# A two-layer hybrid decoder step on eight cores: the program is recorded as a graph and put in order by a list scheduler, the residual becomes token-major, gate sums are scanned

## The reference

```python
for l in range(2):
    hn = rms_norm(h, norm_mix)                       # h: tokens x 1024
    q,k,v,g_out,g_lr,xp,u,vv,gates = split(hn @ w_in)    # 7696 columns
    # A: gated linear attention, 4 heads, state 128 x 256 per head
    g_log = log_sigmoid(g_lr @ w_gk2 + b_gk) / 16
    b = cumsum(g_log)                                # inside a chunk of tokens
    o = (q*exp(b)) @ S + tril((q*exp(b)) @ (k*exp(-b)).T) @ v
    S = exp(b_last) * (S + (k*exp(-b)).T @ v)
    A = (rms_norm(o) * silu(g_out)) @ w_br_a
    # B: trailing window means (2, 4, 8, 16) minus the token, a map per group
    # C: u * (tril(W_s) v + b) in chunks of 128
    h = h + (sig(ga)*A + sig(gb)*B + sig(gc)*C) @ w_out
    h = h + relu(rms_norm(h) @ w_ff1)**2 @ w_ff2     # d_ff = 4096
y = rms_norm(h)
```

## Time and profile before

| | us |
|---|---|
| runs of the kernel (3) | 2885.13, 2886.05, 2887.64; median 2886.05 |
| profiled execution, slowest core (core 4), first to last instruction | 2896.9 |
| spans of the 8 cores in it | 2877.6 to 2896.9 |
| PE busy / its weight loads | 2545.4 (88%) / 1384.2 (48%) |
| DVE / ACT / POOL busy | 1237.7 (43%) / 929.9 (32%) / 75.3 (3%) |
| DMA, HBM read and written | 237.46 MB and 63.96 MB |

### The profile page before, as it was taken

One profiled execution on the slowest core, in us unless ns is written; L12 is line 12 of the kernel. 1 busy time (PEld: TensorE's weight loads), 2 busy tenths in 40 slices (PEclk: granted clock), 3 DMA queues, 4 the chain that ended last, 5 costly groups with the idle time before them and its releaser, 6 DMA issues.

```text
span 2896.9 us, 42207 instructions; the slowest of 8 cores (2877.6 to 2896.9 us)
## 1 busy us (share of the span) xinstructions
PE 2545.4 (88%) x14347; PEld 1384.2 (48%) x14502; DVE 1237.7 (43%) x2227; ACT 929.9 (32%) x1698; POOL 75.3 (3%) x94
## 2 busy tenths in 40 slices
PE   5767967899997899999986797797999889999997
PEld 3434544454543455455443454454455435555554
DVE  4244336434444444444544433553343444444443
ACT  4335545312222211122334454541222231111243
POOL 1000000000000000000000000000000000000000
PEclk6889988999999999999998899898999999999998
DMA  9743071432626211214343307133162621211011
GB/s 242 129 129 112 12 116 44 93 104 62 126 77 134 44 30 30 44 16 81 73 104 113 117 23 110 46 70 115 59 129 77 135 59 16 44 30 30 15 45 80
DMA packets 172520, 225.73 MB, mean 78 GB/s; under 512 B 12242, under 2 KB 159866, under 8 KB 166904
## 3 DMA queue, kind: packets, MB, share of 16 engines
q0 software_dynamic: 80896, 77.97, 19.2%
q1 hardware_dynamic: 91416, 145.06, 15.7%
HBM read 237.46 MB, written 63.96 MB: 104 GB/s over the span
## 4 chain that ended last, share of the span: by engine, by line
PE 77%; DMA 10%; DVE 5%; ACT 4%; issue 3%; SPq 1%; another core or an unknown queue 0%; DVEq 0%; ACTq 0%
PE ps L215 75%; DMA hst<-spool 2%; DMA gla_s<-Sf_77 1%; DVE hn L194 1%; DMA gla_s<-Sf_78 1%; DMA gla_s<-Sf_76 1%; PE ps L224 1%; DMA gla_s<-Sf_79 1%; DMA xt_55<-xp 1%; DMA H4s_110<-H_d 1%; SPq L164 1%; ACT L188 1%; DVE tmp_86 L194 0%; ACT rstd L188 0%; DVE pt_101 L191 0%
## 5 line engine op out<-in xcount | busy, mean ns | idle before, releaser
L215 PE MATMUL ps<-hn,wring 128*128 128x384 bf16 (+1 forms) x6320 | 1251.0, 351 | 13.4 <-DMA wring<-w_in 8.6
L215 PEld LDWEIGHTS ps<-hn,wring 128*128 128x128 bf16 x6400 | 628.0, 99 | 555.3 <-issue 28.8
L188 ACT ACTIVATE rl_124<-ps 128x384 f32<-128x384 f32 (+1 forms) x160 | 85.3, 533 | 502.3 <-PE ps L215 439.8
L215 PE MATMUL ps<-a_1_123,wring 128*128 128x384 bf16 (+1 forms) x1268 | 245.1, 348 | 0.6
L215 PE MATMUL ps<-a_0_122,wring 128*128 128x384 bf16 (+1 forms) x1267 | 241.0, 347 | 0.7
L215 PE MATMUL ps<-wring,hn 128*128 128x512 bf16 x819 | 198.4, 390 | 9.8 <-ACT lv L188 4.1
L215 PEld LDWEIGHTS ps<-a_1_123,wring 128*128 128x128 bf16 x1280 | 125.3, 98 | 108.3 <-issue 2.2
L215 PEld LDWEIGHTS ps<-a_0_122,wring 128*128 128x128 bf16 x1280 | 125.0, 98 | 108.0
L188 ACT ACTIVATE sg_119<-ps 128x384 f32<-128x384 f32 (+1 forms) x120 | 64.0, 533 | 263.8 <-PE ps L215 193.2
L188 ACT ACTIVATE sg_118<-ps 128x384 f32<-128x384 f32 (+1 forms) x120 | 64.0, 533 | 226.4 <-PE ps L215 167.8
L188 ACT ACTIVATE rl_125<-ps 128x384 f32<-128x384 f32 (+1 forms) x160 | 85.3, 533 | 146.3 <-PE ps L215 83.8
(11 more groups left out here) (311 smaller groups left out, 2835.4 us busy)
## 6 DMA issues: line engine op xcount, KB each, us to landing
wring<-w_ff POOLq DMA_DIRECT2D x32, 1024.0 KB, 9.1
wring<-w_in POOLq DMA_DIRECT2D x30, 1024.0 KB, 12.7
OB_d<-OBC SPq DMA_DIRECT2D x6, 768.0 KB, 4.1
H4s_110<-H_d SPq DMA_DIRECT2D x6, 768.0 KB, 12.4
OBs_112<-OB_d SPq DMA_DIRECT2D x6, 768.0 KB, 14.2
H4s_111<-H_d SPq DMA_DIRECT2D x6, 768.0 KB, 13.8
OBs_113<-OB_d SPq DMA_DIRECT2D x6, 768.0 KB, 5.5
h_d<-hT_47 SPq DMA_DIRECT2D x2, 2048.0 KB
```

The source lines that it names most:

```text
L188: return op(ACT, lambda: nc.scalar.activation(out=out, in_=in_, func=func, **kw), reads, writes)
L215: inst = nc.tensor.matmul(m[0], m[1], m[2], start=m[3], stop=m[4], **kw)
```

## The change

Every helper (`act`, `tt`, `pe_group`, `dma` ...) no longer emits its instruction but appends a node to a graph (`record`), with the buffers it reads and writes, a duration and a latency. The code is then written in plain program order without generators, and `schedule()` emits the nodes: again and again, over the five engines, it takes the node that can start first; among those of an engine that can start within 30 ns the one recorded first (an ACT node that needs another table set counts as 60 places later). PSUM banks are given out there too, all eight from one pool.

```diff
-    def op(E, fn, reads=(), writes=()):
-        acquire(E, reads, writes)
-        t = E.tok(fn())
+    def schedule():
+        ...
+                for n in ready[id(E)]:
+                    s = n.ready if n.ready > f else f
+                    key = n.idx
+                    ...
+                    c = (max(s, f + 30.0), key)
+            ...
+            if n.byts:
+                ...
+                dma_at[id(E)] = at0 + (both + alone / 280.0 if alone else n.byts / 140.0)
+                fin = dma_at[id(E)] + 2000.0
```

```diff
+    def rstd_of(src, srcB, junk):
+        act(junk.t[:, :], src, AF.Square, srcB, [junk, s], accum=s.t[:, 0:1])
+        act(s.t[:, 0:1], s.t[:, 0:1], AF.Ln, [s], [s], bias=EPS, scale=1.0 / D)
+        act(s.t[:, 0:1], s.t[:, 0:1], AF.Exp, [s], [s], scale=-0.5)
+    def norm_to_hn(t, src, srcB, junk, stage):
+        s = rstd_of(src, srcB, junk)
+        stt(stage.t[:, :], src, s.t[:, 0:1], wn.t[:, :], ALU.mult, ALU.mult, list(srcB) + [s, wn], [stage])
+        pe_transposes([...  for kt in range(KT)], ident_bf.t[:, :], [stage, ident_bf], [ps])
+        vcopy(hn_v(b)[:, :, j * 128:(j + 1) * 128], ...)
-            pe_group([(ps.t[:, 0:T], ones_bf.t[:, :], s.t[:, 0:T], m == 0, m == KT - 1)], [s, ones_bf], [ps])
```

```diff
-                pe_group([(ps.t[:, j * 128:(j + 1) * 128], lv.t[:, j, h * 128:(h + 1) * 128], cm.t[:, mi, :], True, True)], ...)
+            op(DVE, lambda: nc.vector.tensor_tensor_scan(out=x.t[:, 0:T], data0=rst.t[:, m0:m0 + T], data1=x.t[:, 0:T], initial=0.0,
+                                                         op0=ALU.mult, op1=ALU.add), [x, rst], [x], 2 * T / 0.96 + 90.0, 90.0)
-        plq.dma(wgk2.t[0:16, :], w_gk2[l], writes=[wgk2])
-        plq.dma(wgk2.t[32:33, :], b_gk[l:l + 1, :], writes=[wgk2])
+        for j in range(4):
+            plq.dma(wgk2.t[32 * j:32 * j + 16, :], w_gk2[l], writes=[wgk2])
-            act(sb_.t[:, :, :], s.t[:, :, :], AF.Copy, [s], [sb_])
+                vcopy(sb_.t[:, :, :], s.t[:, :, :], [s], [sb_], E=POOL)
-    Sf = [sba(f"Sf{i}", [128, 2, 256], F32, RA + (6 + 2 * i) * KB) for i in range(4)]
+    Sf = [sba(f"Sf{i}", [128, 2, 256], F32, at(86 + 2 * i)) for i in range(5)]
```

More of the change, by code:

```diff
@@ L96, in release, with __init__ @@
         b.r = {}
+class P(B):
+    def __init__(self, ps_t, allowed):
+        B.__init__(self)
+        self.allowed = allowed
+        self.k = None
+        self.left = 0
+        self.last = 0.0
+        self.t = Late(lambda: ps_t[:, self.k or 0, :])
+class Node:
+    __slots__ = ("E", "fn", "reads", "writes", "late", "occ", "lat", "aset", "idx", "succ", "need", "ready", "tiles", "byts")
 def build_program():
@@ L148, in build_program, with record @@
     POOL = Eng(nc, nc.gpsimd, "pool")
+    nodes = []
+    def record(E, fn, reads, writes, occ, lat, late=(), aset=None, byts=0):
+        n = Node()
+        n.E, n.fn, n.reads, n.writes, n.late = E, fn, tuple(reads), tuple(writes), tuple(late)
+        n.occ, n.lat, n.aset, n.byts = occ, lat, aset, byts
+        n.idx = len(nodes)
+        n.succ = []
+        n.ready = 0.0
+        before = {}
+        for b in n.reads + n.late:
+            for a in b.overlap():
+                if a.lw is not None:
+                    before[a.lw.idx] = a.lw
+        for b in n.writes:
+            for a in b.overlap():
+                if a.lw is not None:
+                    before[a.lw.idx] = a.lw
+                for m in a.lr:
+                    before[m.idx] = m
+        for b in n.reads + n.late:
+            b.lr.append(n)
+        for b in n.writes:
+            b.lw = n
+            b.lr = []
+        before.pop(n.idx, None)
+        n.need = len(before)
+        for m in before.values():
+            m.succ.append(n)
+        n.tiles = list({id(b): b for b in n.reads + n.writes + n.late if isinstance(b, P)}.values())
+        for b in n.tiles:
+            b.left += 1
+        nodes.append(n)
@@ L243, in ps_release @@
[L243 to L271, removed]
-            bg.remove(e)
+            aps += not isinstance(scale, float)
@@ new lines, in act, with vcost, tt @@
+        if accum is not None:
+            kw["accum_out"] = accum
+            aps += 2
+        occ = 0.833 * cols(out) + (60.0 if in_psum(*reads) else 110.0) + 95.0 * aps
+        op(ACT, lambda: nc.scalar.activation(out=now(out), in_=now(in_), func=func, **kw), reads, writes, occ, 125.0, SETS.get(func))
+    def vcost(out, reads, rate=1.0):
+        return cols(out) / 0.96 / rate + 85.0
+    def tt(out, in0, in1, alu, reads, writes, E=None):
+        E = E or DVE
+        occ = vcost(out, reads) if E is DVE else 250.0 + 2.2 * cols(out)
+        op(E, lambda: E.e.tensor_tensor(out=now(out), in0=now(in0), in1=now(in1), op=alu), reads, writes, occ, 90.0)
@@ new lines, in memset, with fn @@
+    def memset(ap, v, writes, E=None):
+        E = E or DVE
+        op(E, lambda: E.e.memset(ap, v), (), writes, vcost(ap, ()), 90.0)
+    def pe_group(mms, reads, writes, late=None):
+        def fn(rs, ws, lt):
+            acquire(PE, rs, ws)
+            inst = None
+            for i, m in enumerate(mms):
+                kw = {}
+                if len(m) > 5 and m[5]:
+                    kw["skip_group_check"] = True
+                if late is not None:
+                    for a in lt[i].overlap():
+                        PE.wait(a.w)
+                inst = nc.tensor.matmul(now(m[0]), m[1], m[2], start=m[3], stop=m[4], **kw)
+            release(PE.tok(inst), list(rs) + list(lt), ws)
+        occ = 0.0
+        for m in mms:
+            n = cols(m[2])
+            occ += max(n / 2.4 * (4 if m[2].dtype == F32 else 1) + 2.5, 60.0)
+        record(PE, fn, reads, writes, occ, 190.0, late=late or ())
@@ L720, in o_view @@
[L720 to L736 removed]
+    cnt2 = [0]
@@ L1099, in build_program @@
-        while smp_e in bg:
-            tick()
+                gla_sample(l)
         mix_prep(l)
```

1089 lines of the change are left out of this document (515 added, 574 removed).

## The result

The changed kernel takes 2517.99 us (median of 5 runs) against 2887.64 (also 5). The ratio is 0.8709, 95% interval 0.8676 to 0.8743. A second set of runs gave 2518.65 us and 0.8696 (0.8684 to 0.8708). The forecast was 2545, with 2475 to 2700 as the range. In some executions the cores of one die run at a lower clock throughout; the first two medians count these, the ratios and every time from here on leave them out.

A forecast was written before the change was run, and what follows sets the result against it. PE-bound in gates and FF, held up by waits elsewhere, 482 us lost. Work 2348 plus losses 60, 37, 64, 6, 8, 6, 7 and 20 gave 2556 us of span, less 10.8: 2545 us, range 2475 to 2700.

The forecast's parts named there:

- Work: PE's work over the whole kernel: from 2415 us, less 97 removed, plus 30 for new bf16 transposes, to 2348 us.
- Start: Loading x and the first weight chunks: DMA-bound at 242 GB/s until 95 us, PE losing 60 us (45 to 80).
- Sample loop and scans: Mixers: PE loses 15 and 22 us in the two layers' sample loops, and 32 us a layer in scans.
- the scans' term: Scans of blocks 2, 3 and 4: DVE's work exceeds PE's, losing 32 us a layer (15 to 50).
- pace: Time between states in the sample loop: DMA sets it, 2.2 us at its bound, 2.5 taken, 2.2 to 2.6 expected.
- Gates, Out, FF: Remaining PE losses in these stages, both layers: 3 us each in gates, 4 each in Out, 6 in FF together.
- Tail: After the last product: only an add, the norm and one store remain, 7 us.
- Clock: Where PE idles its granted clock falls; the mixers stay below 1.00, costing 20 us (5 to 40).
- Rival 1: Waits stay because the build-time order meets late DMAs: 2819 us if all, about 2690 if half; over 2700 chance 0.11.
- sample loop at today's pace: Bound for the sample loop if states come as slowly as before, 3.8 us each: 60 and 67 us lost.
- POOL's cast: Rival 2: the sample loop's cast on POOL sets the pace and slows the kernel, needing 7.8 us a cast; chance 0.02.
- The clock did not give way: Rival 3: dense running on all eight cores lowers PE's clock; time passes 2886 us at share 0.87; chance 0.02.

The follow-up runs named there:

- six buffers: Changed kernel with six state buffers in the sample loop's rotation instead of five, two tiles moved to make room: 2525.1 us, ratio 0.8751.
- flat durations: Changed kernel, scheduler counting 0.5 us per ACT, DVE and SP instruction and multiples of 0.9 us for product groups and POOL: 2645.0 us, ratio 0.9174.
- altered DMA rule: Changed kernel, scheduler counting 3.0 us and 230 GB/s per transfer instead of 2.0 us and 280 GB/s: 2534.84 and 2538.45 us.
- 100 steps: Changed kernel, PE, ACT and DVE at most 100 recorded steps ahead of their own oldest unplaced instruction: 2589.9 us, ratio 0.8973.

## Why the prediction was right, and what was wrong in it

The direction and the mechanism held: PE's work fell as computed, and the waits in gates, Out and FF went. Its sum of 2556 us of span was 39 too long: work 16 too small, clock 25 too small, idle time 80 too large. That these errors have different signs is luck. So is that the time is off by only 27 (2545 against 2518). The sum took off 10.8 us because the profiled execution of before was that much above its median; that belonged to this one execution, and the profiled span of the changed kernel lies 1.3 us below its time.

What the prediction named as signs came: mixers until 453.5 us and 386.5 us long (forecast 460 and 390), gates 294 (297), Out 66 (70), FF 483 and 474 (480), the clock in Out 1.00, the first ring load at 23.2 us (27).

- **Work**, 2348 forecast, 2364 measured, although the narrow gate, which I had priced at full columns, saves some 13 us by itself. What I left out of the price is thus near 30 us; no run says which products they are.
- **Start**, 60 us lost forecast, 47 measured: PE idled 45 of the first 95 us and had done 48 us of work (50.11 x 0.96), where I had put 35. The DMA engines were busy 0.99 of it, as said, but at 186 GB/s, not 242, and PE's last wait for the ring ended at 83.6 us, not 95. The sum behind the 95 mixes two counts: 12.6 MB are six chunks as read, in float32, while the profile's MB and GB/s count what lands, and there a chunk is 1.05 MB. What q0, the casting queue, lands costs more of the engines' time: 7.64 MB in 64.8% of 95 us are 124 GB/s by estimate, q1's 9.93 MB in 33.6% 311 GB/s (113 and 289 in the first 76.7 us of the kernel before, by the rows below). Six chunks, 6.3 MB, at 124 GB/s take 51 us, and 12.6 MB at 242 take 52: two errors that cancelled. The wait for the row copies was there, and it cost nothing.

```profile
q1 hardware_dynamic: 3904, 16.16, 73.0%
q0 software_dynamic: 3389, 2.36, 27.3%
```

- **Sample loop and scans**, 47 us of idle time forecast for layer 0 and 54 for layer 1; measured 18.1 + 11.9 = 30 and 24.7. The step that failed is the scans' term, "42 us of PE work in all against 65 of DVE", 32 us a layer: from 200 to 453.5 us PE idles 11.9. DVE does reach 18.72 us of 20 there, but PE has 17 to 19 us of products beside it. I had counted projections by the place that they have in the program, and the order lays them down by readiness.
- The **pace** of 2.3 us in the middle of layer 0's loop came within the forecast 2.2 to 2.6 for a wrong reason: the rotation of the buffers and not DMA's rate, as six buffers show. Over the whole loops it is 2.9 and 3.4, outside the forecast; in layer 1 half of POOL's waits before a cast end with PE (14 of 29).
- **Gates, Out, FF**, 6 + 8 + 6 us: measured 0.0, 0.9 and 0.2. **Tail** 7: 7.6.
- **Clock**, 20 us forecast (5 to 40), 45 measured, most of it from 95 to 200 us (14) and in layer 1's mixers (22). This is the other step that failed, to the other side: short waits scattered through a stretch cost nearly as much in clock as in idle time (18.1 us idle and 14 in clock from 95 to 200, 24.7 and 22 in layer 1's mixers), while the first 95 us, with 45 idle in a few long waits, cost 2 in clock.
- Two sums of the text are off. Rival 1's 2690 us is half of the *saving* in waits failing to come; half of the loss staying would be 2819 - 241 = 2578. And the sample loop at today's pace would add 90 us (60 and 67 for 15 and 22), not the 67 that the range counts. Neither touches the forecast.

**Rivals.** The waits did not stay. But rival 1 named the right danger: with flat durations 127 us come back, with an altered DMA rule 17 to 20, and one late load in front of a norm costs the slowest core 9.3 us when DVE has the cast. POOL's cast took 0.61 us at its median and set no pace. The clock did not give way: 1.00 from 453.5 to 1296.5 us on all eight cores at once. So the 13/16 of the Trainium skill (TensorE: Matmul & The Clock Gate, Seeing it yourself) is again not what the rows show. Of a price for POOL and DVE at work together there is now a row: km takes DVE 323 ns in the mean with the cast on POOL, and 280 with it on ACT or DVE, so 64 x 43 ns = 3 us of DVE time. The Trainium skill (GPSIMD Engine Reference, Key points) says that GpSimd shares its SBUF interfaces with VectorE and contends with some of its instructions; the rows agree with that, though none tells whether km is one of the kind that it names.

**Where the gain comes from.** The same work, buffers and transfers take 3225 us in recorded order and 2518 in the scheduler's. So the new program needs its scheduler: in the plain order in which it is written it would have been a loss. The kernel before had an order laid by hand (its generators and ticks) and was not run without it, nor under the scheduler, nor the new layout with a hand-laid order. How the 369 us divide between the order and the rest (streamed weights, token-major residual, buffers) is therefore open; by the traces about 50 of them are less work on PE.

## What to carry to other kernels

Write the program as a graph, and let look-ahead, more than exact durations, fill the waits: 100 steps gave 90% of what order could give here, and only the long serial loop needed more. Once the loop was filled from elsewhere, a faster pace, an earlier transfer or a freed queue gave nothing by itself here, though a slower pace still cost. An order fixed at build keeps its queues when a transfer is late: put work that waits for transfers on an engine with nothing urgent behind it, and look at the longest single wait before you explain a loss by a busy share.

## What the runs showed of the hardware

- Products with 32 output columns in four groups of the array overlap: 48 of 384 columns cover 3.7 us, with 128 columns each 11.3.
- DVE's running sum costs 2.05 ns a column ((1215 - 953) / 128), with 953 ns for 384 columns.
- A cast of 128x512 from float32 to bf16 in SBUF takes 420 ns on DVE, 622 on ACT and 677 on POOL in the mean (613 at POOL's median).
- What POOL's queue lands, cast on the way, takes more of the DMA engines' time per MB than the rest: 2.5 times as much in the first 95 us (packets, MB landed, share of 16 engines). The weights are read at twice the size at which they land. Smaller packets (820 bytes against 2900) are not the reason: from 120 to 190 us q1's have 930 bytes, and its 14.14 MB take 66.8% of the engines' time, 302 GB/s of full time against q0's 124. Whether it is the cast or the double reading was not separated.

```profile
q0 software_dynamic: 9326, 7.64, 64.8%
q1 hardware_dynamic: 3407, 9.93, 33.6%
```

- The granted clock can be 0.75 in 20 us of which PE is busy for 18.63; in the 20 us before it PE was busy for 17.73 at 0.99. The busy share of a slice does not tell its clock.
